# Second projection, last token tile: the key and value columns first, and key work buffers of their own

## The chip, the cores and the metric

The kernel is one program on one core of a Trainium2 chip. The metric is the device time of one execution in microseconds (us), lower is better. TensorE (PE in the profile) multiplies matrices into PSUM (the tile `ps`, eight banks of 512 fp32 columns), ScalarE (ACT) and VectorE (DVE) read PSUM and work on SBUF (the tile `arena` and some smaller ones), GpSimd (POOL) and SyncE (SP) mostly issue transfers. The engines run side by side, each through its own instructions in order, and meet at semaphores.

## What is computed

One step of a two-layer backbone on 128 context tokens and 512 latent tokens of width 1024. Layer 0 mixes the tokens with latent attention, layer 1 with grouped-query attention (16 query heads, 4 key and value heads, 64 wide). After each comes a mixture of 16 experts of which a token takes two. The change lies in the start of layer 1:

```python
def gqa_project(h, w_qkv, g_q, g_k):
    qkv = h @ w_qkv                      # (T, 1024) @ (1024, 1536): 1024 query, 256 key, 256 value columns
    q = rms_norm(qkv[..., :nq].reshape(B, T, GQA_HEADS, GQA_HEAD_DIM), g_q)
    k = rms_norm(qkv[..., nq:nq + nk].reshape(B, T, GQA_KV_HEADS, GQA_HEAD_DIM), g_k)
    v = qkv[..., nq + nk:].reshape(B, T, GQA_KV_HEADS, GQA_HEAD_DIM)
...
q_s = apply_rope(q_s, cos_gqa, sin_gqa)
k_s = apply_rope(k_s, cos_gqa, sin_gqa)
mix_s = gqa_attend(q_s, k_all, v_all, gqa_w_o[j])   # softmax over 128 cached and 512 latent keys
```

## The kernel before

The 640 tokens are five tiles of 128 (tile 0 the context, tiles 1 to 4 the latents, `LAT` is 4). For every tile `project` (called by `projection` on TensorE) multiplies the normalised, transposed tile hT by three blocks of 512 columns: queries into PSUM banks 2 and 3, and a third block into bank 4, whose first 256 columns are the keys and whose last 256 are the values. A matmul is two instructions in the trace, so one block of eight is sixteen records. Only after the third block does `project` raise the semaphore `projected`.

ScalarE then copies the 1280 query and key columns out of PSUM (`heads_out`, L912) and the values (L926; for the last tile L950), and squares the former (`squares_g`, L909). VectorE sums the squares by head (`scale_g`, L1191), ScalarE takes a root (`root_g`, L916), VectorE scales (L1197), multiplies by the cosine and sine tables (`times`, L1203) and combines (`rope`, L1042 and L1043), which raises `qk_ready`. TensorE transposes queries and keys (`turn_keys_g`, helper line L1528), and ScalarE copies the transposed queries (L900) and keys (L903) to where the scores read them (`turned_g`, which raises `turned_out`).

The transposes of tile t-1 are done one tile late; for tile 3 they stand between the second and third block of tile 4. The last tile has work of its own in another place: its keys (heads 16 to 19) are treated first, by themselves, and its queries after them. Their tables, rotation and transposes are put into the first steps of the attention loop, since the first steps do not read them. ScalarE's order at the end of the projection is written out by hand: `turned_g(3)`, the wait for `projected`, copy and squares of the keys, copy of the queries, copy of the values, root of the keys, squares of the queries, `turned_g(4)`, root of the queries, a load of the exp table (L955). VectorE's `post_g(4)` does all of the keys, then `scale_g` of the queries, then enters the attention loop.

The attention loop (`heads`) runs 80 steps of head and token tile: scores on TensorE (`score_g`, L1968), a maximum on VectorE (L1077), exp on ScalarE (L695), the scaling of the probabilities on VectorE (L1085), transposes on TensorE (L1528), a copy on ScalarE (L690), and the product with the values on TensorE (`unit`, L1647). The first score waits until `turned_out` says that all key tiles are in place. In the first steps VectorE also does the last tile's rotation, copies its queries (L1141) and sums the modulation of the next part (L991); that sum needs small transfers which ScalarE issues (`mod_fetch`, L651 and L654).

The last tile's two work buffers for squares and table products, `g_last_a` and `g_last_b` (1280 columns each), are picked by `qk_work`. The key part of `g_last_a` lies on the first columns of tile 4's hT, those of `g_last_b` on the end of it.

Of the kernel before, what the change touches and what calls it, by code (L numbers as in the profile page):

```python
# [22 lines left out]
ACT = mybir.ActivationFunctionType  # L23
# [143 lines left out]
def program(nc, ctx, A, O):  # L167
# [8 lines left out]
    def S(name, layer=None):  # L176

        key = name if layer is None else f"{name}_{layer}"
        if key not in sems:
            sems[key] = ctx.enter_context(nc.semaphore(key))  # L180
        return sems[key]
# [71 lines left out]
                split(ps[odd * HD:(odd + 1) * HD, 6 * BANK:8 * BANK], 8))  # L253

    def qk_work(t, i, a, b):
        return ((g_a, g_b), (g_last_a, g_last_b))[t == LAT][i][:, a * HD:b * HD]

    xn = [lambda t, o=o: ar(o + (t % 2) * D, D) for o in (21120, 23040)]
# [347 lines left out]
    def _(act):  # L606
# [13 lines left out]
        def root(name, a, b, batch=0):  # L620

            n = STATS[name][1] + batch + 1
            act.wait_ge(S("mean"), n)
            act.activation(st[:, NTILE + a:NTILE + b], st[:, a:b], ACT.Sqrt).then_inc(S("root"), 1)
# [268 lines left out]
        def turned_g(t):  # L893
            j = t if t > 0 else 5 if t == 0 else 0
            act.wait_ge(S("turned", 1), t + 2)
            if 0 <= t < LAT:
                for half in range(2):
                    for odd in range(2):
                        q_of = split(g_qT[half * HD:(half + 1) * HD], HEADS)[:, odd::2, t * P:(t + 1) * P]
                        act.activation(q_of, split(ps[odd * HD:(odd + 1) * HD, 5 * BANK:7 * BANK], 8), ACT.Copy, scale=SCALE[1])  # L900

            for half, at, n, start in g_keys_of(j):
                last = act.activation(split(g_kT[half * HD:(half + 1) * HD, :], KVH)[:, :, at:at + n],  # L903
                                      split(bank(7)[0:HD, :], KVH)[:, :, start:start + n], ACT.Copy)
            last.then_inc(S("turned_out", 1), 1)

        def squares_g(t, a, b):
            act.wait_ge(S("heads_out"), t + 1 + (t == LAT and a == 0))
            act.activation(qk_work(t, 0, a, b), qk_cols(t, a, b), ACT.Square).then_inc(S("proj_squared", 1), 1)  # L909

        def heads_out(t, a, b):
            return act.activation(qk_cols(t, a, b), ps[:, 2 * BANK + a * HD:2 * BANK + b * HD], ACT.Copy)  # L912
# [6 lines left out]
        for t in range(LAT):  # L919
            act.wait_ge(S("projected"), NTILE + t + 1)  # L920
            if t >= 2:

                act.wait_ge(S("turned", 1), t)
            heads_out(t, 0, HEADS + KVH).then_inc(S("heads_out"), 1)
            j = t if t > 0 else 5
            act.activation(g_V[:, j * NK:(j + 1) * NK], bank(4, NK, NK), ACT.Copy).then_inc(S("proj_out", 1), 1)  # L926
            if t:
                act.wait_ge(S("qk_ready"), t)
            else:
                square_g(LAT)  # L930
            squares_g(t, 0, HEADS + KVH)
            root_g(t + 1, 0, HEADS + KVH)
            if t == 0:
                act.wait_ge(S("qk_ready"), 1)
                act.dma_start(O[3][0, 0, :, 0].rearrange("t h d -> t (h d)"), g_qk[:, NQ:NQ + NK]).then_inc(S("state_stored", 1), 16)
                act.wait_ge(S("proj_out", 1), 1)
                act.dma_start(O[3][0, 0, :, 1].rearrange("t h d -> t (h d)"), g_V[:, 5 * NK:6 * NK]).then_inc(S("state_stored", 1), 16)
            else:
                turned_g(t - 1)
                if t == 1:  # L940

                    act.wait_ge(S("state_stored", 1), 32)
                    root("mix1", LAT, NTILE, 3)
        turned_g(LAT - 1)

        act.wait_ge(S("projected"), 2 * NTILE)
        heads_out(LAT, HEADS, HEADS + KVH).then_inc(S("heads_out"), 1)
        squares_g(LAT, HEADS, HEADS + KVH)
        heads_out(LAT, 0, HEADS).then_inc(S("heads_out"), 1)
        act.activation(g_V[:, LAT * NK:(LAT + 1) * NK], bank(4, NK, NK), ACT.Copy).then_inc(S("proj_out", 1), 1)  # L950
        root_g(NTILE, HEADS, HEADS + KVH)
        squares_g(LAT, 0, HEADS)
        turned_g(LAT)
        root_g(NTILE + 1, 0, HEADS)
# [569 lines left out]
    def _(pe):  # L1524
# [34 lines left out]
        def project(l, t, parts, out_sem):  # L1559

            pe.wait_ge(S("hT_ready"), NTILE * l + t + 1)
            if t:
                pe.wait_ge(out_sem, t)
            for b, (w, cols, landed) in enumerate(parts):
                if b == len(parts) - 1 and t + 1 < NTILE:
                    turn_tile(l, t + 1)
                if l and t == LAT and b == 2:
                    turn_keys_g(LAT - 1)
                if t == 0:
                    pe.wait_ge(*landed)  # L1570
                w = split(w[:, 0:KD * cols], KD)
                for k in range(KD):
                    last = mm(bank(2 + b, cols), hT[l](t)[:, k * P:(k + 1) * P], w[:, k], start=k == 0, stop=k == KD - 1)  # L1573
            last.then_inc(S("projected"), 1)

        def mix(l, it, part):
# [504 lines left out]
```

## Time and profile before

| | us |
|---|---|
| median of three runs | 1373.82 |
| lowest and highest of them | 1367.92, 1375.38 |
| the profiled execution's own time | 1371.09 |
| its span in the trace | 1369.3 |

| engine | busy us | share of the span |
|---|---|---|
| PE | 1256.3 | 92% |
| DVE | 583.9 | 43% |
| ACT | 418.2 | 31% |
| POOL | 55.8 | 4% |

The span is the stretch from the first to the last instruction of one execution. Busy shares are means over stages with different limits; the second projection is the stretch from about 700 to 832 us, the attention loop of layer 1 starts at about 834 us.

### The profile page before, as it was taken

To read this page: it belongs to the slowest core of one execution; us is meant where nothing else is said; L and a number is where in the kernel's file an instruction comes from. 1 tells how busy PE (TensorE), PEld (TensorE's weight loads), DVE (VectorE), ACT (ScalarE), POOL (GpSimd) and SP (SyncE) were. 2 spreads that over 40 slices of the span, in tenths; PEclk is the share of its full clock that TensorE was granted. 3 is DMA by queue.
4 is the path that set the end of the run, shared out by engine and by line. 5 is a ranking of instruction groups with operands and counts; after the bars stand their busy time and mean duration, and the time that the engine had idled before them with its cause. 6 is when DMAs were issued, how large, how long until landed. Compare 5 with 4: busy or idle time off the path is not lost.

```text
span 1369.3 us, 16486 instructions
## 1 busy us (share of the span) xinstructions
PE 1256.3 (92%) x5449; PEld 660.8 (48%) x5449; DVE 583.9 (43%) x1334; ACT 418.2 (31%) x843; POOL 55.8 (4%) x64
## 2 busy tenths in 40 slices
PE   5899899999999999999939996999999999998884
PEld 2455566666664464444414443555444554443331
DVE  1322355444553664222236446677725642212215
ACT  2332344444451121111122336667621211111113
POOL 0102000000000120000020000000000100000002
PEclk9999999999999999999969997999999999999997
DMA  9969999422253067999970004000030469999945
GB/s 375 397 240 414 408 410 414 171 94 94 94 195 134 31 275 263 384 382 371 340 292 9 0 0 190 2 1 1 25 132 31 190 229 374 355 345 343 346 178 216
DMA packets 78545, 299.44 MB, mean 219 GB/s; under 512 B 11817, under 2 KB 29932, under 8 KB 62988
## 3 DMA queue, kind: packets, MB, share of 16 engines
q1 hardware_dynamic: 48096, 206.46, 41.1%
q0 software_dynamic: 16640, 64.56, 12.1%
q10 hardware_dynamic: 13740, 27.52, 5.5%
q8 instruction: 40, 0.66, 0.2%
q14 instruction: 29, 0.24, 0.0%
HBM read 223.79 MB, written 74.73 MB: 218 GB/s over the span
## 4 chain that ended last, share of the span: by engine, by line
PE 76%; SPq 8%; DMA 4%; issue 4%; DVE 4%; ACT 2%; ACTq 1%; DVEq 1%; POOL 1%; POOLq 0%
PE ps L1916 14%; PE ps L1588 10%; PE ps L1573 10%; PE ps L1528 8%; PE ps L1933 6%; PE ps L1806 6%; SPq L468 4%; PE ps L1769 4%; PE ps L1968 3%; PE ps L1621 3%; PE ps L1647 3%; PE ps L1871 2%; PE ps L1543 2%; DMA arena<-in_ada_w 2%; PE ps L1762 2%
## 5 line engine op out<-in xcount | busy, mean ns | idle before, releaser
L1916 PE MATMUL ps<-arena 128*128 128x512 f32 x560 | 246.2, 593 | 0.0
L1528 PE MATMUL ps<-const,arena 128*128 128x128 f32 (+2 forms) x1000 | 157.9, 286 | 58.3 <-DVE arena L1025 19.9
L1528 PEld LDWEIGHTS ps<-const,arena 128*128 128x128 f32 (+2 forms) x1000 | 118.4, 144 | 138.0 <-issue 34.8
L1077 DVE TENSOR_REDUCE hst<-ps 128x1 f32<-128x640 f32 (+1 forms) x160 | 114.7, 717 | 126.3 <-PE ps L1806 89.0
L1573 PE MATMUL ps<-arena 128*128 128x512 f32 (+2 forms) x400 | 156.3, 548 | 8.1 <-DVE arena L1036 4.8
L1916 PEld LDWEIGHTS ps<-arena 128*128 128x128 f32 x560 | 103.9, 190 | 117.2 <-issue 117.1
L690 ACT ACTIVATE arena<-ps 128x640 f32<-128x640 f32 (+1 forms) x160 | 98.9, 618 | 183.9 <-PE ps L1528 169.8
L1588 PE MATMUL ps<-arena 128*128 128x512 f32 x320 | 142.0, 597 | 1.4 <-issue 1.4
L1933 PE MATMUL ps<-arena 128*128 128x512 f32 x280 | 126.1, 593 | 2.2 <-ACT arena L789 2.2
L695 ACT ACTIVATE arena<-ps,hst 128x640 f32<-128x640 f32 (+1 forms) x160 | 112.6, 704 | 20.1 <-DVE hst L1077 19.9
L1573 PEld LDWEIGHTS ps<-arena 128*128 128x128 f32 x400 | 76.4, 195 | 81.6 <-issue 63.9
L1442 DVE STREAM_TRANSPOSE arena<-arena 128x1024 f32<-128x1024 f32 x31 | 62.9, 2027 | 99.7 <-DMA arena<-slot_rows 99.7
L1806 PE MATMUL ps<-arena 128*128 128x320 f32 (+1 forms) x288 | 93.8, 444 | 1.4 <-issue 1.4
L1588 PEld LDWEIGHTS ps<-arena 128*128 128x128 f32 x320 | 59.2, 190 | 69.7 <-issue 69.7
L1933 PEld LDWEIGHTS ps<-arena 128*128 128x128 f32 x280 | 53.1, 190 | 68.6 <-issue 68.6
L1085 DVE TENSOR_SCALAR arena<-arena,hinv 128x640 f32<-128x640 f32 (+1 forms) x160 | 80.0, 500 | 12.8 <-issue 0.4
L781 ACT ACTIVATE arena<-ps 128x256 f32<-128x256 f32 x35 | 13.4, 383 | 229.9 <-PE ps L1916 229.9
L1968 PE MATMUL ps<-arena 64*128 64x320 f32 (+1 forms) x288 | 64.2, 498 | 5.9 <-DVE arena L1141 3.4
L789 ACT ACTIVATE arena<-ps 128x1024 f32<-128x1024 f32 x35 | 35.8, 1023 | 105.6 <-PE ps L1933 105.6
L1806 PEld LDWEIGHTS ps<-arena 128*128 128x128 f32 x288 | 49.0, 191 | 25.3 <-issue 14.3
L1543 PE MATMUL ps<-arena,cond 128*2 128x384 f32 (+2 forms) x528 | 51.3, 515 | 9.8 <-DMA arena<-in_ada_w 8.2
L1448 DVE TENSOR_TENSOR arena<-ps,arena 128x256 f32<-128x256 f32 x35 | 14.5, 413 | 104.7 <-ACT arena L781 104.7
(201 smaller groups left out, 1102.0 us busy)
## 6 DMA issues: line engine op xcount, KB each, us to landing
arena<-in_ada_w SPq DMA_DIRECT2D x62, 768.0 KB, 11.4
slot_rows<-arena POOLq DMA_DIRECT2D x10, 4096.0 KB, 66.2
arena<-in_moe_w_down SPq DMA_DIRECT2D x35, 1024.0 KB, 17.8
arena<-in_moe_w_gate SPq DMA_DIRECT2D x31, 1024.0 KB, 9.2
arena<-in_moe_w_up SPq DMA_DIRECT2D x31, 1024.0 KB, 12.7
slot_rows<-arena ACTq DMA_DIRECT2D x35, 512.0 KB, 8.0
arena<-slot_rows SPq DMA_DIRECT2D x124, 128.0 KB, 11.4
arena<-in_moe_fed SPq DMA_DIRECT2D x8, 1024.0 KB, 9.5
```

The source lines that it names most:

```text
L690: act.activation(pt_out(l, j), split(turned, NB) if l and it else turned, ACT.Copy).then_inc(S("pt_ready"), 1)
L695: act.activation(split(pbuf(l, s, keys), 2 if keys > P else 1), scores(s, keys), ACT.Exp, bias=hst[:, b:b + 1], accum_out=hsum[:, b:b + 1] ...
L1077: nc.vector.tensor_reduce(hst[:, b:b + 1], scores(s, step(s)[3]), AX.XY, ALU.max, negate=True)\
L1085: nc.vector.tensor_scalar(pbuf(l, j, keys), pbuf(l, j, keys), hinv[:, b:b + 1], None, ALU.mult)\
L1528: return nc.tensor.transpose(out, in_, ident[0:rows, 0:rows])
L1543: last = mm(ada_bank(j)[ADA_Q * g:ADA_Q * g + 2, :], c[:, k], w[:, k], start=r == 0, stop=r == KD // ADA_G - 1)
L1573: last = mm(bank(2 + b, cols), hT[l](t)[:, k * P:(k + 1) * P], w[:, k], start=k == 0, stop=k == KD - 1)
L1588: last = mm(bank(mix_bank(it) + half), oT_block(l, k, it), w[:, k], start=k == 0, stop=k == KD - 1)
L1806: last = mm(scores(s, keys)[:, c], m_qT[:, at:at + P], m_kT[:, k:k + w], start=True, stop=True)
L1916: last = mm(split(bank(gu_bank(u)), 2), e_xsT[:, nth(u, D)][:, k * P:(k + 1) * P], w[:, k], start=k == 0, stop=k == KD - 1)
L1933: last = mm(bank(6 + n), e_hidT[:, nth(u, FF)][:, k * P:(k + 1) * P], w[:, k, n * BANK:(n + 1) * BANK], start=k == 0, stop=k == 1)
L1968: last = mm(scores(s, keys)[:, c], g_qT[half, q:q + P], g_kT[half, at:at + w], start=True, stop=True)
```

## The change

It has three parts. TensorE makes tile 4's third block (keys and values) first and raises a new semaphore `last_keys` behind it, then the first query block, the transposes of tile 3, and the second query block, behind which it raises `projected` as before. ScalarE waits for `last_keys` and does the keys' copy, squares and root and the copy of the values before `turned_g(3)`; the queries follow behind it. Since the keys' work now runs while hT of tile 4 is still read, `qk_work` gives it two buffers of 256 columns at the end of the place of tile 3's hT.

```diff
     def qk_work(t, i, a, b):
+
+        if t == LAT and a >= HEADS:
+            return ar(26624 + i * NK, NK)[:, (a - HEADS) * HD:(b - HEADS) * HD]
...
-        turned_g(LAT - 1)
-
-        act.wait_ge(S("projected"), 2 * NTILE)
+        act.wait_ge(S("last_keys"), 1)
         heads_out(LAT, HEADS, HEADS + KVH).then_inc(S("heads_out"), 1)
         squares_g(LAT, HEADS, HEADS + KVH)
-        heads_out(LAT, 0, HEADS).then_inc(S("heads_out"), 1)
         act.activation(g_V[:, LAT * NK:(LAT + 1) * NK], bank(4, NK, NK), ACT.Copy).then_inc(S("proj_out", 1), 1)
         root_g(NTILE, HEADS, HEADS + KVH)
+        turned_g(LAT - 1)
+
+        act.wait_ge(S("projected"), 2 * NTILE)
+        heads_out(LAT, 0, HEADS).then_inc(S("heads_out"), 1)
         squares_g(LAT, 0, HEADS)
...
-            for b, (w, cols, landed) in enumerate(parts):
-                if b == len(parts) - 1 and t + 1 < NTILE:
+            keys_first = l and t == LAT
+            for n, b in enumerate((2, 0, 1) if keys_first else range(len(parts))):
+                w, cols, landed = parts[b]
+                if n == len(parts) - 1 and t + 1 < NTILE:
                     turn_tile(l, t + 1)
-                if l and t == LAT and b == 2:
+                if keys_first and n == 2:
                     turn_keys_g(LAT - 1)
...
+                if keys_first and n == 0:
+                    last.then_inc(S("last_keys"), 1)
```

No instruction is added or taken away on any engine. On TensorE the rows of the built program read the same in both, since the three blocks differ only in the bank and the weights; on VectorE the order does not change. What moves is on ScalarE, at the end of the second projection. L900 and L903 are the copies of transposed queries and keys (of tile 3, and the last L903 of tile 4), L912 the copies out of PSUM, L909 the squares, L950 the values, L916 the roots. Before:

```order
L900 ACTIVATE arena<-ps 64x8x128 [waits turned_1]
L900 ACTIVATE arena<-ps 64x8x128 x3
L903 ACTIVATE arena<-ps 64x4x128
L912 ACTIVATE arena<-ps 128x256 [waits projected]
L909 ACTIVATE arena<-arena 128x256 [waits heads_out]
L912 ACTIVATE arena<-ps 128x1024
L950 ACTIVATE arena<-ps 128x256
L916 ACTIVATE pst<-pst 128x4 [waits proj_mean_1]
L909 ACTIVATE arena<-arena 128x1024 [waits heads_out]
L903 ACTIVATE arena<-ps 64x4x128 [waits turned_1]
L916 ACTIVATE pst<-pst 128x16 [waits proj_mean_1]
```

Now, at the same place (the helpers' lines are three further down):

```order
L915 ACTIVATE arena<-ps 128x256 [waits last_keys]
L912 ACTIVATE arena<-arena 128x256 [waits heads_out]
L950 ACTIVATE arena<-ps 128x256
L919 ACTIVATE pst<-pst 128x4 [waits proj_mean_1]
L903 ACTIVATE arena<-ps 64x8x128 [waits turned_1]
L903 ACTIVATE arena<-ps 64x8x128 x3
L906 ACTIVATE arena<-ps 64x4x128
L915 ACTIVATE arena<-ps 128x1024 [waits projected]
L912 ACTIVATE arena<-arena 128x1024 [waits heads_out]
L906 ACTIVATE arena<-ps 64x4x128 [waits turned_1]
L919 ACTIVATE pst<-pst 128x16 [waits proj_mean_1]
```

Four rows (copy and squares of the keys, the values, the keys' root) went ahead of tile 3's copies and of the wait for `projected`; behind that wait the queries' copy is now the first.

## Rows read from the trace of the kernel before

**Rows 1.** The page, part 4: the chain of work that ended last, by engine.
```profile
PE 76%; SPq 8%; DMA 4%; issue 4%; DVE 4%; ACT 2%; ACTq 1%; DVEq 1%; POOL 1%; POOLq 0%
```
**Rows 2.** Timeline, TensorE: start us, us, what [idle before <-releaser].
```profile
806.31 13.97 PE L1573 MATMUL ps<-arena 128*128 128x512 f32 x32 [0.39 <-ACT arena L926]
...
820.12 1.47 PE L1528 MATMUL ps<-const,arena 128*128 128x128 f32 x12
821.43 7.03 PE L1573 MATMUL ps<-arena 128*128 128x512 f32 x16
832.78 0.62 PE L1528 MATMUL ps<-const,arena 128*64 128x128 f32 x4 [4.32 <-DVE arena L1043]
834.09 1.22 PE L1968 MATMUL ps<-arena 64*128 64x128 f32 x4 [0.68 <-ACT arena L903]
```
**Rows 3.** Timeline, ScalarE, same columns.
```profile
821.63 4.11 ACT L900 ACTIVATE arena<-ps 64x1024 f32<-64x1024 f32 x4 [7.51 <-PE ps L1528]
...
828.50 0.38 ACT L912 ACTIVATE arena<-ps 128x256 f32<-128x256 f32 x1 [2.16 <-PE ps L1573]
828.92 0.42 ACT L909 ACTIVATE arena<-arena 128x256 f32<-128x256 f32 x1
829.24 1.01 ACT L912 ACTIVATE arena<-ps 128x1024 f32<-128x1024 f32 x1
...
830.50 1.05 ACT L909 ACTIVATE arena<-arena 128x1024 f32<-128x1024 f32 x1
833.45 0.59 ACT L903 ACTIVATE arena<-ps 64x512 f32<-64x512 f32 x1 [1.89 <-PE ps L1528]
...
834.55 1.28 ACT L955 ACT_TABLE_LOAD   x1
```
**Rows 4.** Timeline, VectorE, same columns.
```profile
829.37 0.42 DVE L1191 TENSOR_REDUCE pst<-arena 128x4 f32<-128x256 f32 x1 [13.39 <-ACT arena L909]
...
832.44 0.28 DVE L1043 TENSOR_TENSOR arena<-arena 128x128 f32<-128x128 f32 x1
832.82 1.22 DVE L1191 TENSOR_REDUCE pst<-arena 128x16 f32<-128x1024 f32 x1
...
836.20 0.29 DVE L1077 TENSOR_REDUCE hst<-ps 128x1 f32<-128x128 f32 x1
...
854.88 1.02 DVE L991 TENSOR_REDUCE modt<-arena 64x128 f32<-64x512 f32 x1
```
**Rows 5.** Stretches: us, busy us (instructions) of PE, PEld, DVE, ACT, POOL, clock, DMA share, GB/s.
```profile
829.00:834.00 5.00, 0.62 (x4) 0.36 (x4) 3.63 (x9) 3.11 (x6) 0.00 (x0) 0.98 0.90 320
834.00:847.00 13.00, 9.73 (x31) 5.00 (x32) 10.63 (x22) 6.46 (x17) 0.00 (x0) 0.50 0.93 376
848.00:852.00 4.00, 3.41 (x23) 1.89 (x21) 2.63 (x4) 3.98 (x8) 0.00 (x0) 1.00 0.00 0
855.00:861.00 6.00, 6.00 (x22) 3.16 (x22) 3.81 (x8) 1.48 (x3) 0.00 (x0) 0.50 0.02 5
880.00:920.00 40.00, 39.90 (x260) 20.69 (x260) 29.05 (x71) 28.08 (x63) 0.00 (x0) 1.00 0.00 1
```
**Rows 6.** Chain that ended last, attention loop of layer 1: start us, us, what.
```profile
855.00 1.44 PE ps L1968 x4
856.44 1.26 PE ps L1528 x5
857.70 1.05 PE ps L1647 x4
...
889.80 0.74 PE ps L1968 x4
890.54 0.70 PE ps L1528 x5
891.24 0.58 PE ps L1647 x4
```
**Rows 7.** Timeline, ScalarE's transfer queue, and the landing time of these issues.
```profile
844.31 1.00 ACTq L654 DMA_DIRECT2D mod_vec<-in_vec_m  x1
```
**Rows 8.** Transfers between 826 and 870 us: KB each, median us from issue to landing.
```profile
mod_vec<-in_vec_m ACTq DMA_DIRECT2D x2, 32.1 KB, 3.7
```

More of the change, by code:

```diff
@@ L943, in _ @@
                     root("mix1", LAT, NTILE, 3)
+        act.wait_ge(S("last_keys"), 1)
+        heads_out(LAT, HEADS, HEADS + KVH).then_inc(S("heads_out"), 1)
+        squares_g(LAT, HEADS, HEADS + KVH)
+        act.activation(g_V[:, LAT * NK:(LAT + 1) * NK], bank(4, NK, NK), ACT.Copy).then_inc(S("proj_out", 1), 1)
+        root_g(NTILE, HEADS, HEADS + KVH)
         turned_g(LAT - 1)
         act.wait_ge(S("projected"), 2 * NTILE)
-        heads_out(LAT, HEADS, HEADS + KVH).then_inc(S("heads_out"), 1)
-        squares_g(LAT, HEADS, HEADS + KVH)
         heads_out(LAT, 0, HEADS).then_inc(S("heads_out"), 1)
-        act.activation(g_V[:, LAT * NK:(LAT + 1) * NK], bank(4, NK, NK), ACT.Copy).then_inc(S("proj_out", 1), 1)
-        root_g(NTILE, HEADS, HEADS + KVH)
         squares_g(LAT, 0, HEADS)
```

## Prediction

> **What bounds the kernel now.** I read the page's chain first: 76% of the span is TensorE and only a few per cent are VectorE and ScalarE [rows 1]. So a change to those two can only help where TensorE waits for them. The second projection is no such place until its end: tile 4's first two blocks, tile 3's transposes and the third block run with no gap from 806.31 to 828.46 us (821.43 + 7.03) [rows 2]. Behind it TensorE stands idle for 4.32 us, transposes the keys for 0.62 us, waits 0.68 us more, and starts the first scores at 834.09 us [rows 2]. In the stretch from 829 to 834 us it is busy for 0.62 of 5 us [rows 5]. That hole is what the change aims at.
>
> Next, who is late in the hole. ScalarE starts at 828.50 us, right behind the last matmul: keys' copy, keys' squares at 828.92, queries' copy at 829.24, queries' squares at 830.50 [rows 3]. VectorE starts the keys at 829.37 us, right behind their squares, and is done with them at 832.72 (832.44 + 0.28) [rows 4]. Only then, at 832.82, does it sum the squares of the queries, though these were ready at 831.55 (830.50 + 1.05) [rows 3, 4]. Behind that sum come root and scaling, and at 836.20 us the first maximum of the attention loop [rows 4]. The first scores started at 834.09 and took 1.22 us, so they were there at 835.31 [rows 2]: the maximum waits for VectorE itself, 0.9 us longer than for the scores. So the late chain is last matmul, ScalarE, the keys on VectorE, the queries on VectorE, first maximum. From there VectorE goes on almost without a pause, 10.63 of 13 us [rows 5], and carries the extra work of the last queries. Only later does TensorE bound the loop again: from 880 to 920 us it is busy 39.90 of 40 us [rows 5].
>
> **The change part by part.** TensorE's work is the same. The 32 records from 806.31 us are two blocks, 6.98 us each [rows 2]. Now the first is keys and values, and `last_keys` comes at 813.29. Its new place costs nothing on TensorE: the wait ahead of the tile (for the values' copy of tile 3, the last reader of bank 4) is the same wait as before. Tile 3's transposes keep their place after two blocks, at 820.12, and the last block ends at 828.46 as before.
>
> **The keys' work** moves under the matmuls. ScalarE's row at 821.63 has 7.51 us of idle before it [rows 3], so it is free from 814.12 us. Copy and squares of the keys then end at 814.12 + 0.38 + 0.42 and two hand-overs, about 815.0. On VectorE the keys take 3.35 us (829.37 to 832.72), and 13.39 us of idle stand before them [rows 4], so it is free at 815.98. The keys are thus ready at 815.98 + 3.35, about 819.4 us, 9.1 us before TensorE could turn them. The new wait on ScalarE is for `last_keys` (813.29) and, behind it, for VectorE's mean of the keys; queued behind it is `turned_g(3)`, which has no input before the transposes, in the old trace 821.63. So some 4 us of cover lie on that wait. If that cover were gone, ScalarE would still have 2.16 us idle between `turned_g(3)` and the last block's end [rows 3].
>
> **Behind the last matmul** three things are gone from ScalarE's queue: keys' copy, keys' squares and the copy of the values. The queries' copy starts at 828.50 instead of 829.24 us and takes 1.01; the squares follow at a hand-over of 0.04 (the same as between 828.88 and 828.92) at 829.55 and end at 830.60 [rows 3]. VectorE is idle by then and starts the sum at 830.62, with the 0.03 us it also took behind the keys' squares [rows 3, 4]. Before it started at 832.82. **The gain at this point is 832.82 - 830.62 = 2.20 us.**
>
> **What is late next.** TensorE turns the keys at once at 828.5 and is done at 829.1; ScalarE copies them (0.59 us [rows 3]) behind the squares, from 830.62 to 831.21, and the first scores start at about 831.3, at most 1.22 us long, so ready at 832.5 even at the low clock. The first maximum stands at 836.20 - 2.20 = 834.00 us. So the scores do not become the late part. The exp table load (1.28 us, formerly 834.55 to 835.83 [rows 3]) follows the root of the queries, which moves with the sum, so it keeps its distance. TensorE's start moves by 2.8 us and the maximum by 2.2 us, and VectorE decides: 2.20 us are passed on.
>
> **Transfers.** `projected` comes when it came, so the loads behind it stay where they are. ScalarE's small loads for the modulation are issued in the loop, the last at 844.31, landing 3.7 us later, about 848 [rows 7, 8]; VectorE needs them at 854.88 [rows 4]. Issued 2.2 us earlier they fall further into the time in which the large loads fill the queues (DMA share 0.93 to 847 us [rows 5]). Even if they landed no earlier than before, about 4.6 us would be left (854.88 - 2.20 - 848.0). No cost.
>
> **TensorE's clock** is the one cost that the sum leaves open. It stood at 2.4 GHz (0.98 granted) when the hole began and at 1.2 GHz (0.50) from 834 to 847 us, behind the hole; at 2.4 from 848 to 852; at 1.2 again from 855 to 861, behind a pause in which VectorE copied the last queries and summed the modulation; and at 2.4 afterwards [rows 5]. The hole that is left (829.1 to about 834.7, with 0.6 us of scores in it) is nearly as empty as the old one, so I expect the clock to fall again. A loop step on the chain costs 3.75 us at the low clock (1.44 + 1.26 + 1.05) and 2.02 at the high one (0.74 + 0.70 + 0.58), a difference of 1.7 us [rows 6]. How many steps fall on either side is what can move; the bounds are below. I take 0 for it, since the pattern of work and pauses behind the hole is the same.
>
> The Trainium skill ("TensorE: Matmul & The Clock Gate", Part 1: The HAM clock gate) says that the monitor behind this clock runs freely and does not start anew with the work. No single trace shows that. By that rule the rise need not move with the work, which is the first and the third rival; by the row alone (same work, same pattern) the term would be 0.
>
> **The sum.** 0 for TensorE, 0 for the new wait, -2.20 behind the last matmul, 0 for transfers, 0 for the clock: -2.2 us. The profiled execution had 1371.09 us (span 1369.3 and 1.8 around it) and would have 1368.9. It lay 2.7 us below the median of the three runs, which span 7.5 us; on the median, 1373.82 - 2.2 = **1371.6 us**, 0.16% faster.
>
> **Rivals.**
> *The clock keeps its moments and takes half back.* If the rise near 847 us stays while the work is 2.2 us earlier, 2.2 us more of a late stretch are done at half speed, which costs 1.1 us: net -1.1, 1372.7 us. For it: from 834 to 847 us TensorE is busy 9.73 of 13 us, so it carries a part of that chain. Against it: VectorE is busy 10.63 us there and carries more [rows 5].
> *The second low stretch does not occur.* The pause that precedes it might be broken up. The 6.3 us from 855.0 to 861.3 would take some 3.4, 2.9 less: net -5.1, 1368.7 us. For it: the clock was back at 2.4 GHz just before the pause. Against it: the pause is VectorE's work, which the change leaves whole.
> *Slower: the low stretches grow.* The same mechanism the other way. If the rise before the pause is missed and the low clock lasts one step longer behind it, two steps cost 1.7 us more each: +3.4 - 2.2 = +1.2, 1375.0 us. It decides from 1.3 more steps at 1.2 GHz (2.2 / 1.7). Against it: the clock was back by 848 us, and 848 to 852 us shows TensorE busy 3.41 of 4 us at 2.4 GHz [rows 5]; the work ahead of that is the same.
> *It does not do what it says.* The keys would have to miss 828.5 us on VectorE; they have 9.1 us to spare. Then about 0, 1373.8 us.
>
> **How the numbers follow.** Forecast 0.52, half back 0.17, second stretch gone 0.13, slower by a grown low stretch 0.13, no effect 0.05. The likeliest is 1371.6. The range takes the three near cases (1371.6, 1372.7, 1373.8) with the spread of a median around them, and reaches to 1375.0 above; below, to the old low run less the gain, 1367.92 - 2.2 = 1365.7, which takes in 1368.7. So 1366 to 1376. A measurement of this kernel can tell about 0.5%, 6.9 us, from no change. No case above reaches that; what remains is a favourable clock together with the spread of the runs on one side, and a grown low stretch with it on the other: faster 0.05, within 0.5% 0.92, slower 0.03.
>
> **What would show it.** In the profile after: the keys' sum of squares on VectorE at about 816 us and their rotation done by 819.5; one copy and one square on ScalarE between 828.5 and 830.6; the queries' sum at 830.6; first scores at 831.3 and the first maximum at 834.0; and the step of the loop that was at 880 us some 2.2 us earlier. Wrong would be: ScalarE late at `turned_g(3)`, a first maximum that waits for scores or exp, or low stretches of the clock with other lengths than 13 and 6 us, which then explain the rest.

## The result, and the profile after

Over six runs of each the changed kernel took 1364.99 us in the median (1350.62 to 1382.60), the one before 1369.97 us (1367.33 to 1375.38). The ratio is 0.990 with a 95% interval of 0.985 to 0.995. All ratios here leave out, as disturbed, the runs over 1.5% above the fastest of the same kernel; two of the six of the changed kernel went that way, and, as the experiments show, they were the upper part of an ordinary scatter. The medians differ by 5.0 us. I had forecast 2.2 us less, 1371.6 us in a range from 1366 to 1376; 1365.0 lies a microsecond below the range.

The profiled execution took 1367.57 us with a span of 1365.7, against a span of 1369.3 before. First the place that was changed. TensorE's timeline after (start us, us, what, [idle before <-releaser]; the lines of the helpers are a few numbers higher than before):

```profile
820.43 7.03 PE L1579 MATMUL ps<-arena 128*128 128x512 f32 x16
827.30 0.60 PE L1532 MATMUL ps<-const,arena 128*64 128x128 f32 x4
830.28 0.71 PE L1976 MATMUL ps<-arena 64*128 64x128 f32 x4 [2.38 <-ACT arena L906]
```

The last projection block ends at 827.46 us. This program runs 1.00 us ahead of the one before already when it gets here (828.46 there [rows 2]), ahead of anything that the change touches: the last tile's first matmul starts at 805.32 us, where it had been 806.31 [rows 2]. From that matmul to the end of the block it is 22.15 us in all fourteen traces of this text, so the new order of the blocks costs TensorE nothing. All that follows is told from the end of that block. The keys are turned with no pause behind it, where there were 4.32 us of idle [rows 2]. ScalarE after:

```profile
813.16 0.38 ACT L915 ACTIVATE arena<-ps 128x256 f32<-128x256 f32 x1
813.57 0.42 ACT L912 ACTIVATE arena<-arena 128x256 f32<-128x256 f32 x1
813.90 0.36 ACT L950 ACTIVATE arena<-ps 128x256 f32<-128x256 f32 x1
815.77 0.20 ACT L919 ACTIVATE pst<-pst 128x4 f32<-128x4 f32 x1 [1.50 <-DVE pst L1197]
820.63 4.11 ACT L903 ACTIVATE arena<-ps 64x1024 f32<-64x1024 f32 x4 [4.66 <-PE ps L1532]
824.76 0.59 ACT L906 ACTIVATE arena<-ps 64x512 f32<-64x512 f32 x1
827.50 1.02 ACT L915 ACTIVATE arena<-ps 128x1024 f32<-128x1024 f32 x1 [2.16 <-PE ps L1579]
828.56 1.06 ACT L912 ACTIVATE arena<-arena 128x1024 f32<-128x1024 f32 x1
829.64 0.59 ACT L906 ACTIVATE arena<-ps 64x512 f32<-64x512 f32 x1
```

The four short key operations stand where ScalarE had been idle for 7.51 us [rows 3], and 4.66 us of idle are left behind them. Behind the last block only the copy and the squares of the queries remain. VectorE after:

```profile
815.07 0.42 DVE L1195 TENSOR_REDUCE pst<-arena 128x4 f32<-128x256 f32 x1
...
817.80 0.29 DVE L1047 TENSOR_TENSOR arena<-arena 128x128 f32<-128x128 f32 x1
829.65 1.22 DVE L1195 TENSOR_REDUCE pst<-arena 128x16 f32<-128x1024 f32 x1 [11.56 <-ACT arena L912]
...
833.04 0.29 DVE L1081 TENSOR_REDUCE hst<-ps 128x1 f32<-128x128 f32 x1
```

The keys are done at 818.09, 9.4 us before the block ends; VectorE then waits 11.56 us, and the queries' sum starts 2.19 us behind the block instead of 4.36, the first maximum 5.58 us behind it instead of 7.74 [rows 4]. So the hole shrank by 2.17 and 2.16 us.

TensorE's clock, in the stretches that answer to [rows 5] (us, then busy us of PE, PEld, DVE, ACT and POOL, granted clock, DMA share, GB/s):

```profile
834.00:845.00 11.00, 9.60 (x32) 5.17 (x33) 8.79 (x19) 4.82 (x12) 0.00 (x0) 0.50 1.01 404
846.00:852.00 6.00, 3.36 (x19) 1.86 (x18) 4.54 (x8) 4.99 (x8) 0.00 (x0) 0.94 0.01 1
853.00:857.00 4.00, 4.00 (x17) 1.98 (x17) 2.93 (x6) 1.48 (x3) 0.00 (x0) 0.57 0.03 8
857.00:861.00 4.00, 4.00 (x31) 2.48 (x28) 2.50 (x7) 2.54 (x6) 0.00 (x0) 1.00 0.02 4
```

Again two low stretches. The first ends 19.2 us behind the block as it did before (19.0), though the work is 2.2 us ahead. The second ends at 856.9 us, 29.5 behind the block, where it had been 32.7; before, the clock was still low from 855 to 861 us [rows 5].

Last, the expert loop of layer 1, from the first to the last of its 19 gate and up blocks. Before and after, the first block and the last, from TensorE's timelines. Before:

```profile
1108.43 7.03 PE L1916 MATMUL ps<-arena 128*128 128x512 f32 x16
...
1310.99 7.04 PE L1916 MATMUL ps<-arena 128*128 128x512 f32 x16
```

After:

```profile
1103.10 7.03 PE L1924 MATMUL ps<-arena 128*128 128x512 f32 x16
...
1307.98 8.49 PE L1924 MATMUL ps<-arena 128*128 128x512 f32 x16
```

So the account of this pair of traces is: 1.00 us ahead of the change's place, 2.17 in the hole, 2.16 more from there to the first expert block of layer 1 (280.0 became 275.6 us from the block's end, 4.33 less in all), then 2.3 us *lost* in the expert loop (202.6 became 204.9), and 0.6 less behind it: 3.6 us. Only the second of these five terms was in my sum. The experiments ask which of the others belong to the change.

### The profile page after: what moved, and what is told of

It reads as the page before. It is cut to its first block, busy times and chain, and to the rows that moved or that the text cites. A ratio compares the mean times of both kernels' runs of the same rounds, so it can differ in the third digit from the quotient of the medians.

```text
span 1365.7 us, 16486 instructions
## 1 busy us (share of the span) xinstructions
PE 1261.3 (92%) x5449; PEld 663.9 (49%) x5449; DVE 584.2 (43%) x1334; ACT 418.9 (31%) x843; POOL 55.7 (4%) x64
## 4 chain that ended last, share of the span: by engine, by line
PE 78%; DMA 5%; DVE 4%; issue 4%; SPq 4%; ACT 2%; ACTq 1%; POOL 1%; DVEq 1%; POOLq 0%
PE ps L1924 14%; PE ps L1579 11%; PE ps L1596 10%; PE ps L1532 8%; PE ps L1941 7%; PE ps L1814 6%; PE ps L1777 4%; PE ps L1976 3%; PE ps L1629 3%; PE ps L1655 3%; DMA arena<-slot_rows 3%; PE ps L1547 2%; SPq L471 2%; PE ps L1879 2%; PE ps L1770 2%
## 5 line engine op out<-in xcount | busy, mean ns | idle before, releaser
L1532 PE MATMUL ps<-const,arena 128*128 128x128 f32 (+2 forms) x1000 | 160.8, 290 | 51.9 <-issue 19.6
L1579 PE MATMUL ps<-arena 128*128 128x512 f32 (+2 forms) x400 | 155.5, 545 | 9.0 <-DVE arena L1040 4.4
L1814 PEld LDWEIGHTS ps<-arena 128*128 128x128 f32 x288 | 48.9, 191 | 25.4 <-issue 14.3
L1777 PE MATMUL ps<-arena 128*128 128x320 f32 x192 | 57.8, 438 | 0.0
```

Source lines behind the costliest of these rows:

```text
L1532: return nc.tensor.transpose(out, in_, ident[0:rows, 0:rows])
L1777: last = mm(bank(7, QCH), w[:, k, h * P:(h + 1) * P], m_qlT[:, at:at + QCH], start=k == 0, stop=k == 2)
L1814: last = mm(scores(s, keys)[:, c], m_qT[:, at:at + P], m_kT[:, k:k + w], start=True, stop=True)
```

## Experiments

Three theories. **A**: the change takes some 2.2 us out of the hole, all of it is passed on, and the rest is scatter of the transfers and of the clock. **B**: the earlier start brings a steady gain later, as the ratio of 0.99 says. **C**: not the time saved but the new order itself makes the kernel faster. Later a fourth, **D**: the expert loads run on their own clock, so that what is saved ahead of them is not worth its own length.

**The changed kernel again**, unedited, and **the kernel before again**, with a comment added at its end.

> The changed kernel once more. Theory A (the change takes about 2.2 us out of the hole behind the projection, and what else differs between the two traces is spread of the expert loads and of TensorE's clock): from the last projection matmul to the queries' sum of squares on VectorE 2.2 us (before: 4.4), a time about 2.2 us (0.16%) under before, well inside the spread of single runs. Theory B (the shift brings a steady further gain later, as the first comparison's ratio of 0.99 suggests): about 1% faster again, some 14 us, with the attention's output projection of layer 1 again about 5 us earlier relative to before at the first expert of that layer.

> The kernel before, unchanged but for a comment at its end: how far two sets of runs of one program differ. Both theories: no difference. Theory A leans on the spread: single runs of this program should then also scatter by more than the 8 us of the first six, and differences in the expert loop of layer 1 of several us should appear between its own traces. If all its runs agree within 0.3%, theory A loses its main support.

The changed kernel: 12 runs, 1342.46 to 1393.77 us, median 1356.3, ratio 0.9947 (0.9895 to 1.0000). The kernel before under its new name: 12 runs, 1345.43 to 1392.62 us, median 1367.2, ratio to itself 0.9977 (0.9904 to 1.0050). And the 29 runs of before that they share: 1346.79 to 1380.13, median 1368.8. So the program scatters by over 30 us, where I had read 7.5 us off three runs; single comparisons cannot tell 0.2% from 1%. From the last block's end the queries' sum starts at 2.18 us in the changed kernel and at 4.36 in the other, as in the first traces. Theory B's steady 1% isn't confirmed: the second comparison has half of it. Over all runs with full loads the changed kernel has a mean of 1362.1 us (18 runs) and the one before 1365.7 (103 runs): 3.6 less, with a 95% interval (resampled) from 9.8 less to 2.9 more. That can't tell 2.2 us from nothing, and it excludes 1% (13.7 us) only if the chips are taken as one; the runs of the chip of these two sets alone give 6.4 less, from 14.6 less to 2.7 more.

Where the scatter sits is seen in the expert loop. Stretches of 50 us, same columns as above; the kernel before again:

```profile
1150.00:1200.00 50.00, 49.73 (x124) 22.23 (x123) 11.84 (x13) 6.66 (x9) 0.00 (x0) 1.00 1.03 350
1200.00:1250.00 50.00, 40.95 (x98) 17.78 (x97) 11.00 (x12) 5.63 (x8) 0.00 (x0) 0.97 1.04 336
1250.00:1300.00 50.00, 42.14 (x98) 18.02 (x96) 9.86 (x10) 5.63 (x8) 0.00 (x0) 0.97 1.04 317
```

and the kernel of the fourth experiment, whose loop is the same code:

```profile
1150.00:1200.00 50.00, 50.00 (x125) 22.52 (x124) 13.53 (x14) 6.80 (x10) 0.00 (x0) 1.00 1.03 360
1200.00:1250.00 50.00, 47.70 (x118) 20.96 (x117) 12.22 (x15) 6.90 (x10) 0.00 (x0) 1.00 1.03 372
1250.00:1300.00 50.00, 47.99 (x117) 20.90 (x116) 11.04 (x12) 5.63 (x8) 0.00 (x0) 1.00 0.97 354
```

The transfer engines are busy all the time in both, but move 336 and 317 GB/s in one and 372 and 354 in the other, and TensorE is busy for 41 or 48 of 50 us. The loop took 212.5 us in the first and 193.0 in the second.

**The time put back**, and **TensorE's order alone.**

```diff
# e3_after_delay: the changed kernel, and in scale_g
+            for _ in range(3 if t == LAT and a == 0 else 1):
                 nc.vector.tensor_reduce(pst[:, a:b], split(qk_work(t, 0, a, b), b - a), AX.X, ALU.add)
+                settle()
# e4_order_only: the changed kernel, and on ScalarE
-        act.wait_ge(S("last_keys"), 1)
+        turned_g(LAT - 1)
+        act.wait_ge(S("projected"), 2 * NTILE)
...
+        heads_out(LAT, 0, HEADS).then_inc(S("heads_out"), 1)
...
-        turned_g(LAT - 1)
-        act.wait_ge(S("projected"), 2 * NTILE)
-        heads_out(LAT, 0, HEADS).then_inc(S("heads_out"), 1)
```

> The changed kernel with the queries' sum of squares of the last tile made three times over on VectorE (same result), which puts some 2.6 us (2 x 1.22 and the drains between) back into the late chain. Theory A: the first maximum of the attention loop is 2.6 us later against the last projection matmul than in the changed kernel (5.5 becomes 8.1; before had 7.7), and the time is that of before plus 0.4 us. Theory B, if the gain comes from the moment at which the loop starts: also that of before. Theory C (something in the new order itself, not the time saved, makes the kernel faster): still 1% under before.

> TensorE makes keys and values first, but ScalarE keeps its old order and treats the keys only after the last block. Theory A: nothing gained, 7.7 us from the last projection matmul to the first maximum as before, time that of before. Theory C with TensorE's order as the cause: about 1% under before.

VectorE with the time put back; the last projection block of this run ends at 819.59 us:

```profile
821.77 3.81 DVE L1196 TENSOR_REDUCE pst<-arena 128x16 f32<-128x1024 f32 x3 [11.46 <-ACT arena L912]
...
827.79 0.29 DVE L1081 TENSOR_REDUCE hst<-ps 128x1 f32<-128x128 f32 x1
```

The sum starts at 2.18 us, the first maximum at 8.20, 2.62 us later than in the changed kernel, as worked out. The time: median 1363.2 us of 12 runs, ratio 0.9994 (0.9942 to 1.0045). With the order alone the trace reads 4.35 and 7.74 us for sum and maximum, those of before to a hundredth; its last block ends at 822.69 us:

```profile
827.01 0.63 PE L1531 MATMUL ps<-const,arena 128*64 128x128 f32 x4 [4.31 <-DVE arena L1046]
828.32 1.22 PE L1975 MATMUL ps<-arena 64*128 64x128 f32 x4 [0.68 <-ACT arena L906]
```

Its ratio, 1.0109 (1.0012 to 1.0206), rests on four runs from 1352 to 1379 us, which the scatter of before covers; its profiled run has the shortest span of all profiled ones with full loads, 1350.6 us. In the hole, theory C with TensorE's order as the cause is refuted: that order alone changes nothing there. In the whole time four runs can't decide it.

**The scatter taken away.** To see 2 us in the whole time I cut the loads of expert weights inside the loops to their first half; the other half of each buffer keeps an earlier expert's weights, so these kernels leave out half of those loads and compute with other weights. TensorE's work is the same.

```diff
+            n = HALF_SLOT if isinstance(e, int) else HALF_SLOT // 2
             for m, name in enumerate(("moe_w_gate", "moe_w_up")):
-                sp.dma_start(w[:, m], A[name][l][ds(e, 1)].rearrange(rows, p=P)).then_inc(...)
+                sp.dma_start(w[:, m, 0:n], A[name][l][ds(e, 1)].rearrange(rows, p=P)[:, 0:n]).then_inc(...)
```

(and the same for the down weights). Once on one chip:

> The kernel before, with the loads of expert weights inside the expert loops of both layers cut to their first half (the other half of each buffer keeps the weights of an earlier expert; TensorE's work is the same). Theory A holds the loads guilty of the scatter: without them the loops run at TensorE's pace of 10.5 us a tile throughout (before: about 12.3 for the last nine of layer 1), the time falls by 15 to 30 us, and single runs agree within some 5 us instead of scattering over 30 to 45. Theory B makes no statement on the scatter.

> The changed kernel with the same cut in the loads; to be compared with the run e5_light_before beside it. Theory A: 2.2 us less than that one, give or take 1.5 us for TensorE's clock. Theory D (the loads wait for the work, so a saved microsecond is worth more or less than itself where they bind, as the wide comparisons of 0.99 suggest): the difference with light loads is 2.2 too, but with full loads it would be another. Theory B with a cause outside the loads (clock, start moment): 5 us or more less here too.

and again on another:

> The kernel before with the expert loads in the loops cut to their first half, once more, for a second chip. Theory A: around 1348 us with a scatter of some 3 us.

> The changed kernel with the same cut, once more, beside e10_light_before_b. Theory A: 2.2 us less than that one, up to 3.5 us with what TensorE's clock adds, as the traces from the projection's end to the first expert showed (278.5 us in four kernels with the old chain, 274.7 in three with the new). The first pair gave 1.4 less, with a 95% interval from 3.5 less to 0.6 more; theory A wants the two pairs together clear of zero.

| light loads | runs | mean us | lowest, highest |
|---|---|---|---|
| before, first chip | 12 | 1348.5 | 1344.97, 1355.62 |
| changed, first chip | 12 | 1347.1 | 1343.68, 1350.95 |
| before, second chip | 12 | 1350.6 | 1348.09, 1353.49 |
| changed, second chip | 10 | 1345.3 | 1341.78, 1349.80 |

The scatter is gone: the standard deviation of a set is 1.8 to 2.9 us, where full loads gave 7.6 to 15 in every set but the first six runs of before (3.5). The changed kernel is 1.4 us shorter on one chip (interval: 3.5 shorter to 0.6 longer) and 5.3 on the other (6.9 to 3.5). All runs together: **3.2 us shorter, 95% interval 1.8 to 4.7**. That interval takes the two pairs as one, which they are not: they differ by 3.9 us (1.2 to 6.5). So a gain is shown and 1% is excluded, but not the size. The second pair taken alone leaves out the 2.2 us and holds the 5 us of theory B, the first does the opposite.

The traces say where the pairs do not differ. From the last projection block to the first expert block of layer 1 the changed kernel is 3.6 us shorter in both (277.9 to 274.3 and 278.0 to 274.4 us, table below), and the expert loop is equally long in all four. What lies ahead of the block moves more: the block ends 2.9 us later in the first changed trace (828.27 against 825.38) and 5.4 us earlier in the second (822.10 against 827.48). No edit reaches that stretch. With one trace of each kernel it stays open whether such a shift stays with a kernel on a chip, which would explain the two pairs.

The loop with light loads, the kernel before:

```profile
1150.00:1200.00 50.00, 50.00 (x126) 22.49 (x125) 13.95 (x15) 7.04 (x10) 0.00 (x0) 1.00 0.84 246
1200.00:1250.00 50.00, 50.00 (x125) 22.50 (x124) 13.11 (x15) 7.04 (x10) 0.00 (x0) 1.00 0.89 248
1250.00:1300.00 50.00, 50.00 (x124) 22.54 (x123) 10.50 (x13) 6.02 (x9) 0.00 (x0) 1.00 0.67 190
```

TensorE is busy throughout, and the loop takes 187.1 us in each of the light traces, to a tenth. So the full loads cost 6 to 25 us in that loop, another amount in each run. The loop of layer 0 took 155.5 or 155.6 us in each trace, full or light: the loads bind in layer 1 alone.

**The time put back, with light loads.** The edit of e3_after_delay with the cut.

> The changed kernel with the same cut in the loads and the queries' sum made three times, which puts 2.6 us back. Theory A: the time of e10_light_before_b plus 0.4 us, so 2.6 us over e11_light_after_b. Theory C (the new order itself helps): that of e11_light_after_b or 1 us over it.

12 runs, mean 1349.0 us (1344.80 to 1351.99): 3.7 us over e11_light_after_b (1.8 to 5.6), 1.6 under e10_light_before_b (3.1 under to equal). Theory A wanted 2.6 and +0.4; the first is inside the interval, the second just outside. Against C in its strong form it is clear, since putting the time back takes most of the gain away. What may be left is a microsecond or so that isn't the hole. The trace has it too: the first maximum is 0.6 us later than in e10_light_before_b and the first expert block 0.5 us earlier (table below). In between, TensorE's clock rose at 22.5 us behind the block instead of 19.1, and stood at 1.2 GHz for 23.9 us in all instead of 30.7.

**A large dose, full loads.** To see whether time at this place is worth its own length behind the bound loads:

```diff
# e9_dose_full: the kernel before, and in scale_g
+            for _ in range(17 if t == LAT and a == 0 else 1):
                 nc.vector.tensor_reduce(pst[:, a:b], split(qk_work(t, 0, a, b), b - a), AX.X, ALU.add)
+                settle()
```

> The kernel before, full loads, with the queries' sum of squares of the last tile made 17 times (16 more, 1.30 us each with its drain): 20.8 us more in the late chain. Theory A (time at this place is passed on to the end, since the loads of the expert loop start with the work behind it): 20.8 us more than before on the same chip, and the layer-1 expert loop as long as in the other traces (193 to 213 us). Theory D (the loads of that loop run on their own clock and hide part of what is won or lost ahead of them): clearly less than 20.8, say under 12, with a shorter expert loop, near 187 us, since the loads had more time.

```profile
831.84 1.22 PE L1969 MATMUL ps<-arena 64*128 64x128 f32 x4 [0.68 <-ACT arena L903]
855.47 1.44 PE L1969 MATMUL ps<-arena 64*128 64x320 f32 x4 [22.41 <-ACT arena L695]
```

TensorE waits 22.41 us between the first scores and the next, where it had waited 1.79. The first maximum comes 28.79 us behind the projection (7.74 before, so 21.05 more), the output projection 21 us later than before. The time: six runs, mean 1384.1 us, 18.8 more than the 27 runs of before on that chip, interval 12.2 to 25.4. The loop took 194.8 us, not 187. The first load of a chosen expert's weights is issued 272.6 us behind the block, where it had been 251.9, 20.7 us later. The kernel before, then this one:

```profile
1080.40 0.33 SPq L458 DMA_DIRECT2D arena<-in_moe_w_down  x1
```

```profile
1098.40 0.33 SPq L458 DMA_DIRECT2D arena<-in_moe_w_down  x1
```

Theory D, under 12 us, falls, though its bound lies only just outside the interval; the trace says it more clearly: the loads of the loop start with the work and shift with it. The dose does not come alone: the clock stood at 1.2 GHz for 54.6 us up to the first expert block, where it had been 27.3 to 30.7.

**Going on in the same direction.** While TensorE makes the second query block, ScalarE and VectorE are idle again; so the first eight query heads can be treated then.

```diff
# e7_half: the changed kernel, and on ScalarE
...
         root_g(NTILE, HEADS, HEADS + KVH)
+        act.wait_ge(S("last_keys"), 2)
+        heads_out(LAT, 0, PAIR).then_inc(S("heads_out"), 1)
+        squares_g(LAT, 0, PAIR)
         turned_g(LAT - 1)
+        root_g(NTILE + 1, 0, PAIR)
         act.wait_ge(S("projected"), 2 * NTILE)
-        heads_out(LAT, 0, HEADS).then_inc(S("heads_out"), 1)
-        squares_g(LAT, 0, HEADS)
+        heads_out(LAT, PAIR, HEADS).then_inc(S("heads_out"), 1)
+        squares_g(LAT, PAIR, HEADS)
         turned_g(LAT)
-        root_g(NTILE + 1, 0, HEADS)
+        root_g(NTILE + 2, PAIR, HEADS)
# on VectorE
-                scale_g(t, NTILE + 1, 0, HEADS)
+                scale_g(t, NTILE + 1, 0, PAIR)
+                scale_g(t, NTILE + 2, PAIR, HEADS)
# on TensorE, behind each of the first two blocks
-                if keys_first and n == 0:
+                if keys_first and n < 2:
                     last.then_inc(S("last_keys"), 1)
```

> The changed kernel, and beyond it the last tile's queries in two halves: heads 0 to 7 are copied, squared, summed and scaled while TensorE still makes the second query block. Theory A: of copy 1.01, squares 1.05, sum 1.22 and scaling 1.23 us behind the last matmul half goes, about 2.1 us; the first maximum stands 3.4 us behind the last projection matmul (5.6 in the changed kernel, 7.7 in the one before), unless scores become the late part, which stand ready at about 3.5. In time some 4 us under before, hard to see in the scatter.

> The same with the cut loads, to be seen against e5_light_before and e6_light_after: theory A about 4 us under the former and 2 us under the latter. If the first scores take over as the late part, 3 to 4 us and 1 to 2 us.

VectorE in e7_half, whose last projection block ends at 824.77 us:

```profile
817.92 0.69 DVE L1199 TENSOR_REDUCE pst<-arena 128x8 f32<-128x512 f32 x1 [2.54 <-ACT arena L912]
...
826.10 0.69 DVE L1199 TENSOR_REDUCE pst<-arena 128x8 f32<-128x512 f32 x1 [2.21 <-ACT arena L912]
...
827.59 0.69 DVE L1205 TENSOR_TENSOR arena<-arena,pst 128x512 f32<-128x512 f32 x1
828.36 0.29 DVE L1085 TENSOR_REDUCE hst<-ps 128x1 f32<-128x128 f32 x1
```

The first maximum stands 3.59 us behind the block, 1.99 less than in the changed kernel (I had said 3.4). The scores stood ready at 2.7 us, so they don't bind yet. With full loads: 12 runs, median 1359.45 us, ratio 0.9967 (0.9914 to 1.0021). With light loads: six runs, mean 1342.7 us, 4.4 under the changed kernel beside it (2.3 to 6.5) and 5.7 under the one before (3.7 to 8.1). This version beats both where that can be measured, on one chip; how much of the 4.4 is the halves' own is open, since up to the first expert block its trace is only 0.3 us shorter than the changed kernel's (table below).

**All traces between two anchors.** In us from the last projection block's end; "low" is the time that TensorE's clock stood at 1.2 GHz between there and the first expert block, added up from the granted clock of stretches of 1 us. The last column is the expert loop of layer 1.

| kernel | first maximum | output projection | first expert | low | loop |
|---|---|---|---|---|---|
| before | 7.74 | 176.8 | 280.0 | 30.7 | 202.6 |
| e2, before again | 7.92 | 176.6 | 278.1 | 30.7 | 212.5 |
| e4, order only | 7.74 | 176.2 | 277.7 | 27.3 | 193.0 |
| e5, light before | 7.74 | 176.4 | 277.9 | 27.3 | 187.1 |
| e10, light before | 7.91 | 176.5 | 278.0 | 30.7 | 187.1 |
| changed | 5.58 | 175.3 | 275.6 | 23.9 | 204.9 |
| e1, changed again | 5.56 | 173.9 | 274.2 | 20.5 | 207.6 |
| e6, light changed | 5.57 | 172.8 | 274.3 | 20.5 | 187.1 |
| e11, light changed | 5.57 | 174.0 | 274.4 | 20.5 | 187.1 |
| e3, time put back | 8.20 | 176.9 | 278.4 | 27.3 | 204.6 |
| e12, light, put back | 8.52 | 176.0 | 277.5 | 23.9 | 187.1 |
| e7, halves | 3.59 | 172.5 | 274.0 | 23.9 | 196.9 |
| e8, light halves | 3.59 | 172.5 | 274.0 | 23.9 | 187.1 |

The queries' sum starts 4.35 or 4.36 us behind the block in the five traces with the old chain and 2.18 in the four with the new. The first maximum is less even: 7.9 us in e2 and e10, where the clock fell at 2.1 us behind the block instead of 5.4, so that turning the keys took 1.06 us instead of 0.62, and ScalarE does the queries' root only behind its copy of the turned keys.

Two more things stand in the table. To the first expert block the change brings 3.7 us (278.3 on average in the five old traces, 274.6 in the four new ones), 1.5 more than the hole. And the clock is low for 20.5 to 23.9 us instead of 27.3 to 30.7. In each of the five old traces the second low stretch lasts from about 26 to 32.7 or 32.9 us behind the block, in each of the four new ones only to 29.1 to 29.5. Behind it each old trace has two more low stretches, at about 166 and 261 us, and each new one only one, at about 162 us or (e6) at 258.

The second stretch in two rows. In the order-only kernel, whose block ends at 822.69 us, the clock is low from 26.3 to 32.3 us behind it (below); in the changed kernel it is full from 29.5 to 33.5 us (its row from 857 us above):

```profile
849.00:855.00 6.00, 5.75 (x21) 2.97 (x22) 3.79 (x8) 1.48 (x3) 0.00 (x0) 0.50 0.02 5
```

The stretch at 261 us behind the block, before and after:

```profile
1090.00:1096.00 6.00, 6.00 (x17) 4.92 (x18) 4.38 (x25) 0.00 (x0) 1.91 (x2) 0.50 1.03 426
```

```profile
1089.00:1095.00 6.00, 6.00 (x32) 5.30 (x30) 4.01 (x24) 0.00 (x0) 1.90 (x2) 1.00 1.01 419
```

Seventeen matmul records of TensorE fall in the one and 32 in the other. The halves show the limit of this. 1.99 us are won at the first maximum against the changed kernel, the clock rises earlier too (15.6 us behind the block, not 19), but it falls again at 22.4 and comes back at 29.2, and there is a low stretch at 162 us and another at 258. At the first expert block 0.3 to 1.6 us are left. So the clock belongs to the price of a shift, in amounts of the shift's own size. That low time is the cause of the 1.5 us is read off these 13 traces and not shown: no run held the clock up.

## Why the prediction was right, and where it failed

The mechanism was right: what was to leave the chain behind the last matmul left it, by the forecast amount. Two steps failed, the clock's term and the base and range that carry the 2.2 us over to a median of runs.

- **The keys under the matmuls**: right. Ready 9.4 us before the last block ended (forecast 9.1), ScalarE with 4.66 us of idle left behind its new wait (forecast some 4).
- **Behind the last matmul**: right. 2.17 us for 2.20 at the queries' sum.
- **What is late next**: right. The scores started 2.82 us behind the block and weren't waited for, and the maximum moved by 2.16 us (up to 2.35 against e2 and e10).
- **Passed on to the end**: right as far as it can be read. The dose of 21 us came out as 18.8 (12.2 to 25.4), and time put back takes the gain back.
- **TensorE's clock**, taken as 0 because "the pattern of work and pauses behind the hole is the same": wrong. It is the term of the sum that was mis-sized: the traces show 1.5 us of further gain up to the first expert block. The first rival came true and the second by half: the rise near 19 us kept its moment, which takes back, and the second low stretch did not vanish but lasted 3.4 us instead of 6.8, which gives. By the first steps of the loop they nearly cancel: the products that began 32.87 us behind the block (861.33) now begin at 30.54 (858.00), 2.33 less. By the first expert block one of the two later low stretches is missing too, and the gain is 3.7 us instead of 2.2. In the whole time the light pairs give 3.2 us.
- **The base and the range**: the step that put 1365.0 outside. I took the base, 1373.82 us, and the spread, 7.5 us, from three runs of before, and the low end from their lowest less the gain. Over all 103 runs the kernel before has a median of 1367.3 and spreads over 47 us (1345.4 to 1392.6). So the base was 6.5 us too high, and that is nearly all of the 6.6 us by which 1365.0 lies under my 1371.6. That 1365.0 lies 2.3 us under 1367.3, so near to my 2.2, is luck with six runs that scatter over 32 us. And medians of six runs drawn from those 103 lie between 1357 and 1373 in 95% of the draws, so a range of 10 us was too narrow whatever the change did.
- **Where the spread comes from** could have been seen in the trace before. From 1200 to 1300 us TensorE wasn't busy throughout while the transfer engines were, and I didn't look behind the attention loop, since nothing there was changed:

```profile
1200.00:1250.00 50.00, 44.39 (x110) 19.46 (x109) 11.46 (x13) 6.65 (x9) 0.00 (x0) 1.00 1.04 344
1250.00:1300.00 50.00, 43.82 (x107) 19.02 (x106) 11.02 (x12) 5.62 (x8) 0.00 (x0) 1.00 1.04 343
```

My forecast of the sign and of less than 0.5% stands: 3.2 us are 0.24% of 1350. Of the 1% in the first comparison the later runs leave a quarter; the rest is scatter.

## What to carry to other kernels

When an engine has to treat the results of the last block of a stage, make first the columns whose treatment can be finished while the engine makes the others (here the keys, 2.17 us, and then half of the queries, 1.99 more at the first maximum), and cost the gain as the length of what leaves the queue of the *next* engines behind the last matmul, not as the idle time seen (2.17 us of 4.32). Before forecasting a small gain, find the stretch in which transfers bind, even if it lies far from the change: its scatter sets what a whole-kernel measurement can say. And when it says too little, take the scatter's cause away in both kernels alike, on more than one chip, and read the change's own distance between two anchors in the trace; here 2.17 us could be read to 0.02 in every trace while the whole time moved by over 30.

## What the runs showed of the chip that I hadn't expected

The same loads, with the transfer engines busy all the time, moved 317 to 372 GB/s from run to run in the last third of this kernel, and the loop that uses them took 193.0 to 212.5 us with the same code. The loop of layer 0 took 155.5 us in all traces. Why the rate varies was not tried.

TensorE's clock rose and fell at the same moments of the work. In all nine traces of the old and the changed kernel the first rise behind the projection comes 18.9 to 19.3 us behind its last block, while that block itself ended anywhere from 822.1 to 828.5 us of the span. Two of the old ones (e2, e10) fell 3.3 us earlier than the rest, at 2.1 us, and rose with them. The rise stayed where it was although the work came 2.2 us sooner. On this the trace agrees with what the prediction quoted from the Trainium skill ("TensorE: Matmul & The Clock Gate", Part 1: The HAM clock gate), a monitor that runs freely and doesn't start anew with the work.

The equal moments look like the opposite, a monitor that the work sets, but the traces bear out the free one, which the prediction held that no single trace shows. In each of the fourteen traces the clock changes 17 to 27 times, and all these changes, from the first to the last, stand whole multiples of one time apart to within 0.01 us, however long the work between them took. The rises at 15.6 us (halves) and 22.5 us (e12) instead of 19 fit the same spacing. Nor does the work start in step with them: from the first matmul to the fall near 112 us it is 102.4 to 105.5 us in the eight traces that have that fall. It is rather the work that comes into step on its way. From one matmul record of layer 0's attention (the 2001st of the trace, at 352 to 359 us) to the clock's fall near 690 us it is 331.2 to 331.5 us in eleven traces and 329.8 to 330.0 in the other three. From the 2901st record, in the expert loop of layer 0, it is 127.8 to 128.2 in all fourteen. In between the eleven pass a low stretch 140 us behind the first of these matmuls, and their work takes 1.5 us longer; the three have none there. So the clock's part in a small change need not be noise, although the monitor is free. That such stretches are what brings the work into step is my reading of these numbers; no run tried it.
